# The second token half is turned ahead of the third pass of the first half's products, at ten norms

## The reference

```python
for l in range(DEPTH):        # first kind
    x = x + 0.5 * swiglu(rmsnorm(x, ffn1_norm[l]), w_ffn1_in[l], w_ffn1_out[l])
    u = rmsnorm(x, mix_norm[l])
    ...
    x = x + merged @ w_out[l]
    x = x + 0.5 * swiglu(rmsnorm(x, ffn2_norm[l]), w_ffn2_in[l], w_ffn2_out[l])
for l in range(L):            # second kind
    x = _layer_norm(DN_ALPHA * x + 0.5 * _swiglu(x, ffn1_w1[l], ffn1_w2[l]), ln1_g[l], ln1_b[l])
    mix = _token_mix(x, w_in[l], ...)
    x = _layer_norm(DN_ALPHA * x + mix, ln2_g[l], ln2_b[l])
    x = _layer_norm(DN_ALPHA * x + 0.5 * _swiglu(x, ffn2_w1[l], ffn2_w2[l]), ln3_g[l], ln3_b[l])
```

## Time and profile before

| | kernel before |
|---|---|
| median of three runs | 2684.05 us |
| lowest, highest | 2679.64, 2684.26 us |
| the profiled execution | 2684.22 us |
| its span | 2682.4 us |
| granted TensorE clock, mean over the span | 0.996 |
| busy: TensorE, its weight loads | 2639.6, 2422.1 us |
| busy: VectorE, ScalarE, GpSimd | 867.2, 1287.7, 2033.4 us |

### The profile page before, as it was taken

How to read it: one execution, slowest core, us unless ns; L and a number is a source line. 1 busy time by engine, 2 the same in 40 slices (tenths; PEclk the granted TensorE clock), 3 DMA queues, 4 the chain that set the end, 5 groups by cost and what they waited for, 6 DMA issues and landing times.

```text
span 2682.4 us, 46928 instructions
## 1 busy us (share of the span) xinstructions
PE 2639.6 (98%) x19082; PEld 2422.1 (90%) x19082; DVE 867.2 (32%) x1516; ACT 1287.7 (48%) x1898; POOL 2033.4 (76%) x906
## 2 busy tenths in 40 slices
PE   8999999999999999999999999999999999999998
PEld 6989999899899989989989998998998989899897
DVE  2644354211232425421121133732122131473212
ACT  4435555444444555544444445744444444574443
POOL 7878655888888856688888886468888878537886
PEclk9999999999999999999999999999999999999999
DMA  6555533555556553655555555245555545524554
GB/s 230 188 180 197 184 123 127 195 185 186 209 181 196 198 181 126 158 196 184 186 200 184 178 189 205 88 154 197 185 181 199 189 165 201 177 96 166 196 183 139
DMA packets 128733, 474.70 MB, mean 177 GB/s; under 512 B 14432, under 2 KB 14432, under 8 KB 127520
## 3 DMA queue, kind: packets, MB, share of 16 engines
q1 hardware_dynamic: 124704, 454.09, 49.4%
q0 software_dynamic: 3840, 17.82, 2.2%
HBM read 469.23 MB, written 2.62 MB: 176 GB/s over the span
## 4 chain that ended last, share of the span: by engine, by line
PE 93%; DVE 2%; DMA 2%; ACT 1%; POOL 1%; issue 0%; SPq 0%; DVEq 0%; ACTq 0%; POOLq 0%
PE psA L378 52%; PE psY L378 38%; PE psT L429 3%; DMA ring<-in_weights 2%; POOL rest L1040 1%; ACT upper L1843 0%; DVE psY L1254 0%; DMA cst<-in_consts 0%; DVE x L1269 0%; DVE psY L1242 0%; ACT xT_upper L1843 0%; ACT G L1874 0%; DVE Sc L1745 0%; DVE arena L1443 0%; DVE st L1260 0%
## 5 line engine op out<-in xcount | busy, mean ns | idle before, releaser
L1040 POOL TENSOR_TENSOR rest<-ring,upper 128x1024 fp32r<-128x1024 f32 (+1 forms) x834 | 1993.0, 2411 | 587.7 <-ACT upper L1843 577.3
L1843 ACT ACTIVATE upper<-ring 128x1024 fp32r<-128x1024 f32 (+1 forms) x834 | 868.5, 1052 | 773.9 <-DMA ring<-in_weights 772.3
L378 PE MATMUL psA<-xT_rest,upper 128*128 128x256 f32 x2784 | 391.4, 283 | 0.0
L378 PE MATMUL psA<-xT_upper,upper 128*128 128x256 f32 x2784 | 389.7, 282 | 0.6 <-ACT arena L1843 0.6
L378 PE MATMUL psA<-xT_upper,rest 128*128 128x256 f32 x2784 | 383.6, 280 | 0.0
L378 PEld LDWEIGHTS psA<-xT_upper,upper 128*128 128x128 f32 x2784 | 364.9, 189 | 14.0 <-ACT arena L1843 1.3
L1295 DVE TENSOR_TENSOR psA<-sil,psA 128x256 f32<-128x256 f32 x144 | 61.8, 429 | 961.5 <-ACT sil L1843 961.4
L378 PEld LDWEIGHTS psA<-xT_rest,upper 128*128 128x128 f32 x2784 | 359.9, 192 | 0.0
L378 PEld LDWEIGHTS psA<-xT_upper,rest 128*128 128x128 f32 x2784 | 352.9, 189 | 0.0
L378 PE MATMUL psY<-upper,hT_rest 128*128 128x512 f32 x704 | 205.3, 397 | 0.0
L378 PE MATMUL psY<-upper,hT_upper 128*128 128x512 f32 x704 | 203.9, 395 | 0.7 <-DVE hT_rest L1297 0.7
(11 more groups left out here) (277 smaller groups left out, 3102.1 us busy)
## 6 DMA issues: line engine op xcount, KB each, us to landing
ring<-in_weights SPq DMA_DIRECT2D x862, 512.0 KB, 3.4
G<-in_rows POOLq DMA_DIRECT2D x6, 1024.0 KB, 7.6
G<-in_rows POOLq DMA_DIRECT2D x7, 512.0 KB, 6.0
arena<-rel_by_distance POOLq DMA_DIRECT2D x8, 256.0 KB, 8.2
x<-in_x SPq DMA_DIRECT2D x2, 512.0 KB, 5.9
par<-in_params POOLq DMA_DIRECT2D x4, 256.0 KB, 5.8
xn<-in_mem POOLq DMA_DIRECT2D x1, 1024.0 KB, 9.3
memory_transposed<-arena POOLq DMA_DIRECT2D x1, 1024.0 KB, 5.0
```

The source lines that it names most:

```text
L378: i = pe.matmul(out, lhsT, rhs, start=start, stop=stop)
L1040: pool.tensor_tensor(rest[:, r, 0:n], ring[:, r, 0:n], upper[:, r, 0:n], ALU.subtract)\
L1843: act.activation(out, in_, func, **kw).then_inc(*up)
```

## The change

In `by_halves` the call that turns the second token half moves from behind the third pass of the first token half to ahead of it. Nothing is added or removed: the eight transposes, with their two waits for the scaled half, stand in TensorE's queue ahead of eight matmuls that stood ahead of them. The other queues are as before. The third pass still reads the first half's columns of xT_upper and goes on filling the same PSUM bank.

```diff
@@ -460,12 +460,12 @@
                 for i in range(4):
                     for q in range(2):
                         mm(out, xT[1][:, 2 * i + q, 0:P], parts[i][1][0][:, q], False, False)
+                turn_half(norm, 1)
                 for i in range(4):
                     pe.wait_ge(*sig["rest parts"].after(("piece", parts[i][0])))
                     for q in range(2):
                         mm(out, xT[0][:, 2 * i + q, 0:P], parts[i][1][1][:, q], False, (i, q) == (3, 1),
                            filled(label + (0,)) if (i, q) == (3, 1) else None)
-                turn_half(norm, 1)
                 out = fill(pe, banks[1], label + (1,))
                 for i in range(4):
                     if i % 2 == 0:
```

## The result

The changed kernel took 2694.69 us in the median of five runs (2687.24 to 2695.04), the kernel before 2680.99 us in its five (2679.64 to 2684.26). The medians are 13.7 us apart, the means 10.6 us; the ratio is 1.004, with a 95% interval of 1.0027 to 1.0053. In a second set, six runs beside twelve of the kernel before, it was 1.0049 (1.0036 to 1.0061). So the change costs 7 to 16 us. The forecast of 2694.7 us was made from a median of 2684.05; in this and the later sets of runs the kernel before stands some 3 to 5 us lower (medians of 2679.2 to 2681.0), so the forecast of the difference, 10.7 us, is what is to be judged, not the agreement in the last digit.

What follows compares the result with a forecast made beforehand. The prediction took TensorE's instruction stream plus its gaps as the bound. Losses of 4.7, 4.3 and 3.1 us less norm 0's 1.4 gave +10.7 us, 2694.7 us from a median of 2684.05; range 2687 to 2701.

Steps and rivals of the forecast that it cites:

- E and s: At each norm: E, start of the third pass's first matmul before the change; s, start of VectorE's second-half scaling, claimed unmoved.
- s + 1.97: At the nine norms behind the first: earliest start of the matmul after the eight waiting transposes; bounds s + 1.6 and s + 2.1.
- s + 4.32: At the nine norms: the second half's third matmul, after 1.97 us of turn, 1.88 of third pass and 0.47 of two matmuls.
- +1.16 to +1.18: Loss at each RMS norm (2, 3, 5, 6), worked out as +1.18 us at norm 2; four together +4.7 us.
- the signs: Expected in the changed trace: TensorE idle about 1.5, 1.7 and 2.5 us ahead of the transposes, 9 more waits for scaling.
- Norm 0: At the start of the kernel: the transposes fill TensorE's wait for POOL's last split, a gain of 1.38 us.
- Passing it on: Downstream of each norm: TensorE has no gap to take the delay in, so it is handed down in full.
- the later weight splits: Behind ScalarE's SiLU or bank copy: splits start later by about TensorE's own delay; counted as nothing, bounds 0 and 0.5 us each.
- rival (a): Clock falls in TensorE's new gaps, near 3 us per fall; two falls give 2701 us; chance 0.12.
- (b): Scaled residual is there in time at all norms, third matmul at E + 3.22; 2676.3 us, faster; chance 0.05.
- (c): Delay is taken in later by waits on transfers or POOL; 2684 to 2687 us, no change; chance 0.06.
- (d): Only part of the loss: shorter waits for s or some norms' chains speeding up; 2688 to 2691 us; chance 0.07.

Runs made afterwards that it cites:

- the filled gap: Changed kernel with eight useless 128x512 matmuls ahead of the transposes at norms 8 and 11; median 2688.3 us beside 2693.0 for the changed kernel, ratio 1.0040.
- the changed kernel again: The changed kernel unaltered, run once more beside the kernel before; ratio 1.0049 (1.0036 to 1.0061).
- the transposes that needn't wait: Changed kernel, but at the nine norms behind the first the early transposes read the first half's tokens, long scaled; ratio 0.9954 to the kernel before.
- norm 0 alone: Kernel before with the second half's turn moved ahead of the third pass at norm 0 only; ratio 0.9995 (0.9986 to 1.0005).
- The split turn: Changed kernel, but at nine norms four transposes stand ahead of the third pass's last pair, four behind it; ratios to the kernel before 0.9988 and 0.9986.
- the last pair: Changed kernel, but at nine norms all eight transposes stand ahead of the third pass's last pair of matmuls; ratio to the kernel before 1.0001 (0.9992 to 1.0010).

## Why the prediction was right

**The two times, E and s.** The method held. Where the transposes of the nine norms wait for the scaling they stand at s + 0.80 or s + 0.81 (at s + 0.85 or 0.86 at seven norms of the filled gap, where the wait for the bank has moved ahead of them too), else behind the work in front of them. The order doesn't move s: it comes 2.50 us behind the start of the second pass before and 2.48 after at norm 2, 2.80 and 2.78 at norm 7, 3.55 and 3.56 at norm 8.

**The wait.** s + 1.97 for the start of the third pass was 0.09 us too late: 1.88 was measured. The third pass with the first pair behind it took 2.41 us where 2.35 was taken. The sum, s + 4.32, was 0.03 us off; +1.16 to +1.18 became +1.15, +1.42 to +1.44 became +1.40, +1.54 became +1.51. Two of the signs were off: TensorE's idle times are 1.3, 1.5 and 2.3 us, each 0.2 shorter than forecast, since the profile counts them from the end of the last matmul and I counted from the start that the next one would have had; and the list has 8 more waits instead of 9, as norms 8 and 11 had theirs already and norm 0 got one.

**Norm 0.** -1.38 against -1.37, with the rests beside the split at no cost: they took 0.69 us each, as alone. That is the rule of the Trainium skill's page SBUF — State Buffer, "Who interferes with whom", for VectorE with one operand in SBUF, and the trace agrees.

**Passing it on.** That later stages hand the delay down in full is shown by the distances: norm 2 to norm 3 is 189.99 us before and 191.15 after, 1.16 longer; norm 2's own loss is 1.15. So the later weight splits, which I counted at nothing, took nothing there.

**The clock.** The forecast counted nothing for it; rival (a) did, and it came in part. Both gaps of 2.3 us in the profiled execution had a fall, but I took 3 us for each, and 1.3 and 1.5 us were measured, since the low clock held in only part of the transposes and the pass. The chance of 0.12 was too small: in the traces six of eight such gaps had one. What misled me was a row that I read wrongly. Rows 6 have weight loads idle for 2.51 us, and I wrote that the first half's matmuls went on at the full pace behind it. They didn't. The kernel before started at half pace, ahead of that wait and behind it:

```profile
10.37 1.97 PE L429 MATMUL psT<-cst,xn 128*128 128x128 f32 x8 [10.37 <-DMA cst<-in_consts]
...
18.10 2.88 PE L378 MATMUL psA<-upper,xT_rest 128*128 128x512 f32 x8
```

Eight transposes took 1.97 us, as at the low clock in rows 7 (1.94) and not as in rows 3 (1.04), and the second pass took 2.88 us, against 2.00 at norm 2. The profile prints a granted clock of 1.00 for this stretch, so here only the durations tell. A clock that is low already can't fall. In one trace of the twelve, that of the changed kernel again, the first matmuls behind the same wait ran at the full pace (a pair in 0.74 us, against 1.22), and 2 us later the granted clock was at 0.50:

```profile
15.09 0.74 PE L378 MATMUL psA<-upper,xT_upper 128*128 128x512 f32 x2 [1.80 <-ACT upper L1843]
...
17.87 3.26 PE L378 MATMUL psA<-upper,xT_rest 128*128 128x512 f32 x8
```

```profile
18.00:20.00 2.00, 2.00 (x6) 1.54 (x5) 2.00 (x2) 0.00 (x0) 2.00 (x1) 0.50 0.00 0
```

So rows 6 were no evidence against (a). The forecast of 10.7 us meets the 10.5 of the order, which is what it was a sum of; that the two profiled spans differ by 10.7 us as well is luck, as 2.8 us of clock behind norms 8 and 11 and 3.7 us of a slow stretch that was missing stand against each other in it.

**Rivals.** (b) fell with s, and its price, 3.22 us from E, was met by the transposes that needn't wait. (c) fell: nothing took the delay in. (d) didn't occur.

## What to carry to other kernels

An operation that waits in an in-order queue should stand where its input comes, not as early as its consumers would like: put just enough independent work ahead of it to reach that time, and keep the rest behind it to cover what follows. Read the time of the input against the end of the work in front, place by place; one source line that runs in ten places had a gain at one, losses of three sizes at nine, and for seven of the places the best order of those tried was neither of the two. A gap in TensorE's stream, here one of 2.3 us, costs more than itself when the clock falls behind it, here 1.2 to 1.6 us more. And before a stretch of a trace is taken as a case in which the clock did not fall, see from the length of like instructions that it was high there.

## What the runs showed of the hardware that I had not expected

Whether one more VectorE copy in layer 0 runs long decides over as much time as this edit at norms 8 and 11, or more. The timelines of the kernel before (first) and of norm 0 alone (second) show such a copy and the GpSimd split beside it; behind the copies of this stage wait TensorE's transposes, 3.75 us in rows 7 and 1.47 us in the last line:

```profile
133.43 4.85 POOL L1040 TENSOR_TENSOR rest<-ring,upper 128x1024 fp32r<-128x1024 f32 x2
133.45 2.52 DVE L1444 COPY arena<-arena 32x256 f32<-32x256 f32 x1
```

```profile
132.28 0.28 DVE L1448 COPY arena<-arena 32x256 f32<-32x256 f32 x1
132.32 5.08 POOL L1044 TENSOR_TENSOR rest<-ring,upper 128x1024 fp32r<-128x1024 f32 x2 [0.22 <-ACT upper L1847]
...
137.31 1.23 PE L429 MATMUL psT<-cst,xn 128*128 128x128 f32 x8 [1.47 <-DVE arena L1465]
```

Where the split starts 0.02 us ahead of the copy, the copy takes 2.52 us, about the length of a split; where it starts 0.04 us behind, 0.28 us. Four copies of this stage, two of 32x256 and two of 128x256 numbers, take either 0.3 or 2.3 to 2.5 us each. In eight traces two of them were long: the wait is 3.6 to 4.0 us, and the clock fell behind it each time. In the other four one was long: the wait is 1.5 us, and the clock never fell. From the scaling at norm 0 to that at norm 2 it is 482.9 to 483.6 us in these four, and 486.4 to 488.4 us in the six of the eight that have the early turn at norm 0 as these four do. The split turn and the last pair, traced twice each, had one outcome once and the other once, so it isn't the edit; it is probably a good part of the spread of the runs (2672.15 to 2684.79 us for 29 runs of the kernel before). The page SBUF — State Buffer of the Trainium skill, "Who interferes with whom", says that a VectorE copy in its two-port mode and a GpSimd operation exclude each other for a whole instruction, the first to start winning. The durations and starts above agree with it; what shifts the two starts against each other was not tried.
